# The third branch's schedule: one projection beside each step, V turned inside the projection behind, the first scores inside the last tile of keys

## The reference

```python
proj = jnp.einsum('bsd,dc->bsc', h, w_in)
aq, ak, av, az, buv, bz, cq, ck, cv, cz, gl = split_cols(proj)
...
qc = partial_rope(cq.reshape(B, S, C_HEADS, C_HEAD_DIM), positions)     # 8 heads of 64
kc = partial_rope(ck.reshape(B, S, C_HEADS, C_HEAD_DIM), positions)
vc = cv.reshape(B, S, C_HEADS, C_HEAD_DIM)
for window, dil in C_PATTERNS:                                          # (128,1), (512,4), (2048,16)
    o_p, lse_p = dilated_window_attention(qc, kc, vc, window, dil)
wts = jax.nn.softmax(jnp.stack(lses, axis=0), axis=0)
oc = jnp.sum(wts[..., None] * jnp.stack(outs, axis=0), axis=0)
yc = oc.reshape(B, S, C_WIDTH) * jax.nn.silu(cz)
...
gates = jax.nn.sigmoid(gl.reshape(B, S, N_BRANCH, D))
merged = jnp.einsum('bsnd,nbsd->bsd', gates, pb)
return x + jnp.einsum('bsd,de->bse', merged, w_out)
```

## Time and profile before

| | |
|---|---|
| median of three runs | 3769.11 us (3768.09 to 3772.36) |
| the profiled execution | 3772.45 us, of which 3770.7 us from its first to its last instruction |
| mean granted TensorE clock | 0.979 of full |
| TensorE matmul busy | 3598.6 us (95%) |
| VectorE, ScalarE, GpSimd busy | 1875.5 (50%), 1355.3 (36%), 1090.8 us (29%) |
| third branch, first layer | about 755 to 1163 us of the span |
| third branch, second layer | about 2021 to 2425 us |

### The profile page before, as it was taken

How to read it: one execution, slowest core, us unless ns; L and a number is a source line. 1 busy time by engine, 2 the same in 40 slices (tenths; PEclk the granted TensorE clock), 3 DMA queues, 4 the chain that set the end, 5 groups by cost and what they waited for, 6 DMA issues and landing times.

```text
span 3770.7 us, 49460 instructions
## 1 busy us (share of the span) xinstructions
PE 3598.6 (95%) x19870; PEld 3187.6 (85%) x19870; DVE 1875.5 (50%) x3550; ACT 1355.3 (36%) x2965; POOL 1090.8 (29%) x794
## 2 busy tenths in 40 slices
PE   6999999999998999999999999999999999999998
PEld 5888887878887788888877888778999999999998
DVE  5444555256556453155535565555434546424543
ACT  3212444045553121044422555523235532225641
POOL 2633322322222354322322222223531013531102
PEclk9999999999999999999999999999999999999999
DMA  3122111411114311211123111242210012211012
GB/s 108 44 77 67 40 34 45 148 42 45 45 45 146 123 51 56 82 34 43 45 90 106 45 40 45 95 157 64 63 49 24 29 63 87 71 51 35 25 41 94
DMA packets 85476, 244.80 MB, mean 65 GB/s; under 512 B 10752, under 2 KB 24832, under 8 KB 85248
## 3 DMA queue, kind: packets, MB, share of 16 engines
q1 hardware_dynamic: 85248, 241.66, 19.4%
HBM read 191.09 MB, written 50.53 MB: 64 GB/s over the span
## 4 chain that ended last, share of the span: by engine, by line
PE 75%; DVE 13%; ACT 6%; issue 3%; DMA 1%; POOL 1%; SPq 0%; DVEq 0%; POOLq 0%; ACTq 0%
PE pj L1569 28%; PE pS L1569 27%; PE po L1819 4%; PE pS L1799 3%; PE pS L1801 2%; PE pS L1663 2%; PE pS L1664 1%; DVE tmp L2496 1%; PE po L1711 1%; DVE KK L2508 1%; DVE tmp L2499 1%; PE po L1685 1%; PE pj L1811 1%; DVE tmp L2493 1%; DVE tmp L2489 1%
## 5 line engine op out<-in xcount | busy, mean ns | idle before, releaser
L2990 POOL TENSOR_SCALAR Whi<-stage 128x1024 fp32r<-128x1024 f32 (+3 forms) x252 | 261.5, 1038 | 1855.9 <-PE pj L1569 923.7
L1569 PE MATMUL pj<-Hhi,Whi 128*128 128x512 f32 x1576 | 629.1, 399 | 5.6 <-issue 5.6
L1569 PE MATMUL pj<-Hhi,Wlo 128*128 128x512 f32 x1576 | 617.9, 392 | 0.0
L1569 PE MATMUL pj<-Hlo,Whi 128*128 128x512 f32 x1576 | 616.9, 391 | 0.0
L2992 POOL TENSOR_TENSOR Wlo<-stage,Whi 128x1024 fp32r<-128x1024 f32 (+3 forms) x252 | 598.3, 2374 | 21.0
L1569 PE MATMUL pS<-Hhi,Whi 128*128 128x512 f32 x856 | 343.4, 401 | 24.0 <-DVE Hlo L2361 13.6
L1569 PEld LDWEIGHTS pj<-Hhi,Whi 128*128 128x128 f32 x1576 | 299.1, 190 | 67.1 <-issue 6.0
L1569 PEld LDWEIGHTS pj<-Hhi,Wlo 128*128 128x128 f32 x1576 | 297.5, 189 | 64.0
L1569 PEld LDWEIGHTS pj<-Hlo,Whi 128*128 128x128 f32 x1576 | 298.3, 189 | 57.5
L1569 PE MATMUL pS<-Hlo,Whi 128*128 128x512 f32 x856 | 340.5, 398 | 0.0
L1569 PE MATMUL pS<-Hhi,Wlo 128*128 128x512 f32 x856 | 340.2, 397 | 0.0
(11 more groups left out here) (485 smaller groups left out, 8041.5 us busy)
## 6 DMA issues: line engine op xcount, KB each, us to landing
stage<-wstream SPq DMA_DIRECT2D x228, 512.0 KB, 3.5
merged<-Mb SPq DMA_DIRECT2D x32, 512.0 KB, 2.9
Mb<-merged SPq DMA_DIRECT2D x32, 512.0 KB, 5.3
gates<-tmp SPq DMA_DIRECT2D x48, 256.0 KB, 2.2
TH<-gates SPq DMA_DIRECT2D x24, 512.0 KB, 6.2
xres<-X SPq DMA_DIRECT2D x16, 520.0 KB, 2.9
xr<-xres SPq DMA_DIRECT2D x16, 520.0 KB, 3.7
X<-xT SPq DMA_DIRECT2D x16, 256.0 KB, 6.7
```

The lines of the kernel that those rows point to most:

```text
L1569: x = pe.e.matmul(ps, w[a][:, v.koff + k * P:v.koff + k * P + P], moving(v.of, b, k, v.t0, v.n), start=k == 0 and i == 0, stop=k == v.K - ...
L2990: pool.e.tensor_scalar(upper, stage, 1.0, 0.0, ALU.mult, ALU.add).then_inc(*pool.tick("whi", c))
```

## The change

The first tile is no longer prepared ahead of step 0 in one piece. `attention_c` now runs Q's first half, K's first half, Q's second half, then K's second half with the first scores inside it behind k = 4; the first softmax stands in the list ahead of that last unit. They use two banks, since `NARROW` is set before. V's units of every tile, the first too, stand in step 0 of their own tile. The turns of V use the bank pt in place of a projection bank: the first stands inside V's second unit (behind k = 5), the second inside Z's first unit (behind k = 3). Steps 0 to 7 hold 2, 1, 1, 1, 1, 1, 3 and 2 units: Z is in steps 1 and 2, the first two gates in 3 and 4.

```diff
             def turned(u):
...
-                vtok[buf][u.i] = (u.emptied, u.id)
+                vtok[buf][u.i] = (out, u.id)
+                if not diff:
+                    u["free"], self.pt_free = self.pt_free, (out, u.id)
...
-        (q0, q1), (k0, k1) = qk_units(0, {(x, i): None for x in "qk" for i in range(2)})
-        self.run([q0, q1, k0, k1])
-        self.run(v_units(0))
...
-        scores(0)
-        scored[0]["free"] = self.bank_free[2:6]
+        free = self.bank_free[2:6]
+        (q0, q1), (k0, k1) = qk_units(0, {(x, i): None for x in "qk" for i in range(2)})
+        self.run([q0, k0, q1])
+        k1["inside"] = {4: [scores(0, True)]}
+        scored[0]["free"] = free
         soft(0)
-        fresh, turned = [], []
+        self.run([k1])
+        v = v_units(0)
         for s, (j, h, i) in enumerate(steps):
...
-                amid = [fresh + z[0:1] + turned, z[1:2], g[0:1], g[1:2], [], g[2:3], g[3:4], []]
+
+                for u in v[2:]:
+                    u["within"] = True
+                v[1]["inside"], z[0]["inside"] = {5: v[2:3]}, {3: v[3:4]}
+                amid = [v[0:1] + v[2:3] + v[1:2], v[3:4] + z[0:1], z[1:2], g[0:1], g[1:2], g[2:3], g[3:4], []]
                 if j < 3:
                     read, v = [], v_units(j + 1)
                     q, k = qk_units(j + 1, {(x, i): read for x in "qk" for i in range(2)})
                     amid[6], amid[7] = [q[0], g[3], k[0]], k[1:2]
-                    fresh, turned = v[0:3], v[3:]
...
+        bank = m.pt if u.bank is None else m.pj[u.bank]
         for c in range(4):
-            x = pe.e.transpose(m.pj[u.bank][:, c * P:c * P + P], m.tmp[u.i][:, c * P:c * P + P], ident[:, :])
+            x = pe.e.transpose(bank[:, c * P:c * P + P], m.tmp[u.i][:, c * P:c * P + P], ident[:, :])
```

More of the change, by code:

```diff
@@ L723, in turned @@
                 self.tmp_free[u.i] = ("v_turned", u.id)
-                vtok[buf][u.i] = (u.emptied, u.id)
+                vtok[buf][u.i] = (out, u.id)
+                if not diff:
+                    u["free"], self.pt_free = self.pt_free, (out, u.id)
             out = "v_out" if diff else "v_low"
             return (self.in1("value", l, COL[br + "v"] + j * P, box={}, sets=sets, emptied="v_copied")
-                    + [Unit(kind="v_turn", i=i, buf=buf, banked=True, sets=turned, diff=diff, emptied=out)
+                    + [Unit(kind="v_turn", i=i, buf=buf, banked=diff, sets=turned, diff=diff, emptied=out if diff else None)
                        for i in range(2)])
@@ L768, in attention @@
             return
+        (q0, q1), (k0, k1) = qk_units(0, {(x, i): None for x in "qk" for i in range(2)})
+        self.run([q0, q1, k0, k1])
+        self.run(v_units(0))
         steps = [(j, qb) for j in range(4) for qb in range(8)]
@@ L1986, in v_turn @@
     def v_turn(u):
-        src, tiles = m.pj[u.bank][:, :].rearrange("p (a b) -> p a b", a=4), slice(4 * u.i, 4 * u.i + 4)
+        src = (m.pt if u.bank is None else m.pj[u.bank])[:, :].rearrange("p (a b) -> p a b", a=4)
+        tiles = slice(4 * u.i, 4 * u.i + 4)
         act.wait_ge(("v_turned", u.id))
@@ L2646, in v_turn @@
             return
-        src, tiles = m.pj[u.bank][:, :].rearrange("p (a b) -> p a b", a=4), slice(4 * u.i, 4 * u.i + 4)
+        src, tiles = m.pt[:, :].rearrange("p (a b) -> p a b", a=4), slice(4 * u.i, 4 * u.i + 4)
         for x in u.rel:
```

## The result

The changed kernel takes 3745.3 us in the median of four runs (3744.22 to 3751.36), the kernel before 3770.74 in the same session (3768.09 to 3775.65): ratio 0.9934, 95% interval 0.9917 to 0.9952. The forecast was 3750 us, and faster. The profiled execution took 3745.62 us, 26.8 less than the one of before; the forecast had a gain of 19.6.

The account below looks back on a forecast made before the run. The prediction took TensorE, busy 95% of the span, to bound the kernel. Its terms, 37.3 - 7.8 - 5.3 - 4.6 = 19.6 us gain, put the forecast at 3750 us, with its own range 3742 to 3760, widened by rivals to 3739 to 3763.

Parts of the forecast that it names:

- Step 4: In each tile's step without projections, adding one removes TensorE's waits and their clock price: gain 37.3 us in all.
- Rival B: The projection in step 4 hides only waits ahead of the product; step 5's turn still waits: 3771, no change, chance 0.08.
- The passage: From tile to tile, V's turn waits 2.7 us for its copy: loss 1.3 us, six times, 7.8 in all.
- The clock at the passages: At the tile-to-tile passages, idle time makes TensorE's clock fall at three of six, 1.75 us each: cost 5.3 us.
- Rival A: The clock holds at all six tile-to-tile passages and the branch's start costs nothing: gain 29.5 us, 3740, chance 0.2.
- The start: At the branch's start VectorE's rotations set the pace and delay scores and P's turn: loss 2.3 us per layer, 4.6.
- Rival C: Slower: V's turn at tile-to-tile passages becomes a new hole, decisive from 5.5 us a passage; at 6.7, 3777; chance 0.06.

Follow-up runs that it names:

- e1: The kernel before with only the projection lists evened (step 4 filled, Z one step later), V's turns and the start as they were: 3745.7 us, ratio 0.9944.
- e3: The changed kernel with V's first unit listed ahead of step 1's softmax and step 7's output, so ScalarE copies it earlier: 3739.61 us, ratio 0.9924.
- e5: The changed kernel run once more, unaltered, for a second look at its clock: 3744.06 us, ratio 0.9929.
- e7: The changed kernel with V's first unit moved to the end of step 7, its turn earlier and listed ahead of the softmax: 3730.99 us, ratio 0.9898.
- e4: The changed kernel with the first softmax listed ahead of Q's second unit, so the mask follows two rotations: 3739.75 us, ratio 0.9929.
- e9: Against e7, V's second turn listed ahead of step 2's softmax, inside Z's first unit behind its second chunk: 3731.92 us, ratio 0.9901.
- e2: The changed kernel with the lists undone (step 4 empty again), V's turns inside the projections and the new start kept: 3775.16 us, ratio 1.0023.

## Why the prediction was right

The direction and the mechanism held. The sum was too low: 26.8 us by the profiles, where 19.6 were forecast. Of these 7.2 us, 4.0 lie outside the branch and are no effect of the change. Inside it one term was too large, one too small, and both misses are the clock's in the main.

- **Step 4: right.** Forecast 16.61 us from product 3 to product 5, measured 16.55; gain 4.9 for a tile of the first layer, 4.5 in the second, 37.6 in all, where 37.3 were forecast. No wait above 0.1 and a clock of 1.00. Rival B (the turn of step 5 waits as before) is refuted by the same rows. e1 shows that the lists alone carry the change, 0.9944 without the rest of it.
- **The passage: right.** Forecast a wait of 2.7 for the copy and 0.4 for the low halves, measured 2.63 and 0.24; loss 1.3 at each, measured 1.33 to the product of step 0 (17.60 against 21.73 less a projection of 5.46) and 1.36 to that of step 1. e3 shows the cause that was only argued: the copy's place in ScalarE's queue. What I had not seen is in e1: 0.9 of it comes with the move of Z alone. I had charged it all to the turn's new place.
- **The clock at the passages: a term too large.** I took three of six at 1.75, 5.3 us. It fell at one of six in the first trace and at two in e5, and lengthened the way to the product of step 1 by 0.8, and by 1.1 and 1.0 us: 0.8 in the one execution, 2.2 in the other. The step that failed is the reading of the earlier trace rows: a stretch of 2.3 went either way there, I made it one in two, and I took the price from step 4, where two waits stand close together. Rival A's full clock came at five and at four of the six passages, its free start did not.
- **The start: the mechanism right, the size partly by luck.** Forecast 2.3 in each layer, measured 55.44 + 5.5 - 58.35 = 2.6 and 54.92 + 5.5 - 56.66 = 3.8, and in e5, in the same way, 2.5 and 2.4. The scores waited 1.94 (forecast 2.4). In the first layer the turn came 1.1 late, at 786.46, forecast 785.4: two rotations beside a split took 6.95 and 7.5 us, where I had 6.7 and 6.3. The low parts cost most of it (774.56: 2.80 for two, 780.84: 3.92 for two; 0.69 each with no split beside them, as after the first rotation). That the loss grew by only 0.3 is luck: I took the same clock again behind the turn, and it was better, 0.85 over the 15.11 us to the product of step 0, 4.5 us at 1.2 GHz, where it had been 0.68 over 9.64, 6.2 us. In the second layer the turn came as forecast, 30.4 us behind the branch's start, and the 3.8 is the clock's. From that turn to the product of step 0, in the first trace and in e5:

```profile
2037.35:2053.27 15.92, 15.77 (x59) 12.50 (x59) 6.56 (x16) 6.11 (x15) 0.51 (x1) 0.80 0.11 33
2035.34:2049.92 14.58, 14.43 (x60) 11.53 (x60) 6.55 (x16) 6.13 (x15) 0.51 (x1) 0.88 0.10 36
```

- **Outside the branch.** From its first projection to its last product the branch gained 12.9 us in the first layer and 9.9 in the second, 22.8. By the terms above it is 37.6 - 8.9 (five passages at 1.33, one at 2.2) - 6.4 = 22.3. The other 4.0 of the profile's 26.8 come from stretches that the change doesn't touch, and these vary by as much from one execution to the next: behind the branch's second layer it takes 1347.5 us before, 1344.2 in the changed kernel, 1347.5 in e1 and 1351.4 in e7. The medians differ by 25.4, with an interval of 18 to 31, and can't tell these 4.0 from nothing.
- **Rival C** (a passage dearer than 5.5 us) is off: the dearest, with its fall of the clock, cost 2.5.

## What to carry to other kernels

A hole in front of one instruction is best filled with work that stands elsewhere for free, and its worth is read from the whole stretch between two fixed points, not from the sum of its waits: that way the clock's price comes in by itself. The second point must lie far enough behind: from product to product of steps 7 and 0 e1 looked like the full change and e3 like a gain of 1.3, while the falls of the clock stood in the step behind. A reader that waits for a copy often waits for the copy's place in its engine's queue. Moving it forward then brings only what the next wait in the chain leaves: 1.3 of 2.6 us in e3 (and the clock took it back at three of six places), 1.3 of 6.2 in e4, nothing of 1.6 in e9; filling the hole with V's own projection, in e7, brought 6.4. Before such an edit, read who is late second.

## What the runs showed of the hardware

**VectorE's operations on two SBUF operands slow up to four times beside a weight split.** A 64x512 TENSOR_TENSOR of VectorE between SBUF operands takes 0.69 us alone. With the second half of GpSimd's 128x1024 split beside it (the TENSOR_TENSOR of 2.7 us), two took 2.80 to 3.92, and in e7's trace one took 2.12 where it takes 0.69 elsewhere; the split's second half ran there from 885.66 to 888.38:

```profile
886.81 2.12 DVE L2319 TENSOR_TENSOR Ylo<-tmp,Yhi 64x512 fp32r<-64x512 f32 x1 [0.69 <-ACT Yhi L1874]
```

In the branch's two layers of the changed kernel's trace the multiplication by the sine, 128x512 with both operands in SBUF, took 2.61 to 2.63 us six times beside such a half and 0.67 to 0.69 otherwise. Operations with an operand in PSUM took what they always take: the low part of P out of pt, 128x512, 0.69 in all 32 cases, ten of them beside a split; and this mask, which takes 0.29 at 784.79 with no split beside it:

```profile
2035.68 0.29 DVE L2631 CUSTOM_DVE_ANT_0 P<-pS,mask 128x128 f32<-128x128 f32 x1
2035.19 2.67 POOL L3003 TENSOR_TENSOR Wlo<-stage,Whi 128x1024 fp32r<-128x1024 f32 x1
```

The Trainium skill, "GPSIMD Engine Reference", section 1, "Specifications", says that GpSimd shares its SBUF interfaces with VectorE, with contention for VectorE's instructions that have two SBUF inputs. The traces agree, and add the price.

**A fall of the clock can shorten a later wait.** The same program waited 6.19 us ahead of P's first turn in one layer and 3.44 in the other. The five microseconds from the first scores on, in the first and in the second layer:

```profile
777.50:782.50 5.00, 2.76 (x13) 2.05 (x13) 4.03 (x6) 2.23 (x4) 1.98 (x2) 1.00 0.24 87
2029.50:2034.50 5.00, 4.35 (x13) 3.25 (x13) 3.54 (x6) 2.19 (x4) 0.43 (x1) 0.66 0.26 92
```

Where the clock held, K's unit ended early, the next weight split started at 780.43 and ran beside both of Q's low parts. Where it fell to half behind the scores' wait of 1.97 us, the split came 1.4 later, measured from the branch's start, and met only one of them:

```profile
2032.88 0.68 DVE L2517 TENSOR_TENSOR QL<-tmp,QQ 64x512 fp32r<-64x512 f32 x1 [0.69 <-ACT QQ L1983]
2034.19 1.46 DVE L2517 TENSOR_TENSOR QL<-tmp,QQ 64x512 fp32r<-64x512 f32 x1 [0.63 <-ACT QQ L1983]
```

All eight starts of this form in four traces (the changed kernel twice, e2, e3) go by this: in two, both in the first layer, the clock of that window is 1.00 and the wait is 6.18 or 6.19; in six it is 0.63 to 0.66 and the wait is 3.44. That the split is the link is read from these rows; no run moved the split by itself.
